# Expert activations of a two-block model: turned on TensorE before the store, or on VectorE after the load

## The reference

```
s1, i1 = top_k(q . sub_keys[0], 16);  s2, i2 = top_k(q . sub_keys[1], 16)
top_s, pos = top_k(s1 + s2, 16);      expert = (i1 * 128 + i2)[pos];  g = softmax(top_s)
u = u_emb[expert];  a = gelu(einsum('thkd,td->thk', u, xb));  coef = g * a
out = einsum('thk,thkd->td', coef, v_emb[expert])
```

## Time and profile before

| | |
|---|---|
| runs | 4169.63, 4172.17, 4174.17 us; median 4172.17 us |
| profiled execution | span 4171.1 us from first to last instruction; its own time lies 1.07 us under the median if measured from the span alone, and no other time of it is given |
| busy share of the span | PE 99%, weight loads 85%, DVE 74%, ACT 55%, POOL 12% |
| chain that ended last | PE 94%, DVE 4%, ACT 1% |
| HBM | 199 GB/s over the span |

### The profile page before, as it was taken

How to read it: one execution, slowest core, us unless ns; L and a number is a source line. 1 busy time by engine, 2 the same in 40 slices (tenths; PEclk the granted TensorE clock), 3 DMA queues, 4 the chain that set the end, 5 groups by cost and what they waited for, 6 DMA issues and landing times.

```text
span 4171.1 us, 72720 instructions
## 1 busy us (share of the span) xinstructions
PE 4116.5 (99%) x21876; PEld 3527.9 (85%) x21876; DVE 3099.3 (74%) x5278; ACT 2278.5 (55%) x4043; POOL 516.1 (12%) x509
## 2 busy tenths in 40 slices
PE   8999999999999999999999999999999999999998
PEld 8978898888888888888889899988888888888887
DVE  6476677885999766777769978688599985566666
ACT  5446544555666655555554465455566665555554
POOL 4100010000222211111100002000022221111110
PEclk9999999999999999999999999999999999999999
DMA  6434656666666666777765545576666666667664
GB/s 223 163 121 150 202 175 194 207 207 197 191 192 191 201 220 219 231 261 246 239 212 178 176 153 184 163 210 206 199 193 190 190 198 221 216 218 238 216 219 161
DMA packets 310247, 831.31 MB, mean 199 GB/s; under 512 B 29040, under 2 KB 129136, under 8 KB 306800
## 3 DMA queue, kind: packets, MB, share of 16 engines
q1 hardware_dynamic: 305184, 812.76, 61.4%
q10 hardware_dynamic: 4944, 17.06, 1.2%
HBM read 779.37 MB, written 50.33 MB: 199 GB/s over the span
## 4 chain that ended last, share of the span: by engine, by line
PE 94%; DVE 4%; ACT 1%; issue 1%; DMA 0%; DVEq 0%; SPq 0%; ACTq 0%
PE psum L419 11%; PE psum L417 11%; PE psum L418 11%; PE psum L485 11%; PE psum L487 11%; PE psum L486 11%; PE psum L1717 5%; PE psum L1719 5%; PE psum L1718 5%; PE psum L1909 2%; PE psum L1911 2%; PE psum L1910 2%; PE psum L408 1%; DVE sb_w_lo L2297 1%; PE psum L426 1%; PE psum L1815 1%
## 5 line engine op out<-in xcount | busy, mean ns | idle before, releaser
L2297 DVE TENSOR_TENSOR sb_w_lo<-sb_raw,sb_w_hi 128x512 fp32r<-128x512 f32 x2736 | 1887.1, 712 | 986.5 <-ACT sb_w_hi L1998 975.5
L1998 ACT CAST sb_w_hi<-sb_raw 128x512 fp32r<-128x512 f32 x2736 | 1696.9, 623 | 1581.2 <-PE psum L487 645.0
L417 PE MATMUL psum<-sb_w_hi,sb_act_hl 128*128 128x512 f32 x2048 | 811.4, 396 | 1.1 <-DVE sb_w_lo L2297 1.1
L419 PE MATMUL psum<-sb_w_lo,sb_act_hl 128*128 128x512 f32 x2048 | 801.5, 391 | 0.0
L418 PE MATMUL psum<-sb_w_hi,sb_act_hl 128*128 128x512 f32 x2048 | 798.9, 390 | 0.0
L485 PE MATMUL psum<-sb_w_hi,sb_act_hl 128*128 128x512 f32 x2048 | 797.0, 389 | 0.8 <-DVE sb_w_lo L2297 0.8
L486 PE MATMUL psum<-sb_w_lo,sb_act_hl 128*128 128x512 f32 x2048 | 796.7, 389 | 0.0
L487 PE MATMUL psum<-sb_w_hi,sb_act_hl 128*128 128x512 f32 x2048 | 796.7, 389 | 0.0
L1717 PE MATMUL psum<-sb_act_hl,sb_w_hi 128*128 128x256 f32 x1488 | 429.8, 289 | 26.9 <-DVE sb_w_lo L2297 13.8
L419 PEld LDWEIGHTS psum<-sb_w_lo,sb_act_hl 128*128 128x128 f32 x2048 | 385.0, 188 | 82.1
L485 PEld LDWEIGHTS psum<-sb_w_hi,sb_act_hl 128*128 128x128 f32 x2048 | 384.4, 188 | 81.0 <-DVE sb_w_lo L2297 1.2
(11 more groups left out here) (377 smaller groups left out, 4240.2 us busy)
## 6 DMA issues: line engine op xcount, KB each, us to landing
sb_raw<-in_u SPq DMA_DIRECT2D x512, 512.0 KB, 4.2
sb_raw<-in_v SPq DMA_DIRECT2D x512, 512.0 KB, 3.5
sb_raw<-in_w_z SPq DMA_DIRECT2D x82, 512.0 KB, 4.3
sb_raw<-in_w_gates SPq DMA_DIRECT2D x64, 512.0 KB, 3.6
sb_acts_in<-acts_mid SPq DMA_DIRECT2D x256, 128.0 KB, 3.3
acts_mid<-sb_acts_out SPq DMA_DIRECT2D x126, 256.0 KB, 5.4
sb_raw<-in_w_proj SPq DMA_DIRECT2D x56, 512.0 KB, 4.2
sb_raw<-in_w_q SPq DMA_DIRECT2D x48, 512.0 KB, 3.8
```

The costliest lines, as they stand in the source:

```text
L417: pe.matmul(ps, h, w_hi[:, c, :], start=k == 0, stop=False)
L419: return pe.matmul(ps, h, w_lo[:, c, :], start=False, stop=k == 15)
L1998: act.copy(w_hi[:, c, :], raw[:, 2 * par + c // 2, (c % 2) * 512:(c % 2) * 512 + 512]).then_inc(hi_ready, 1)
L2297: dve.tensor_tensor(w_lo[:, c, :], raw[:, 2 * par + c // 2, (c % 2) * 512:(c % 2) * 512 + 512], w_hi[:, c, :].bitcast(F32), ALU.subtract). ...
```

## The change

ACT writes the gelu of group g into `up_acts` (both t), SP stores that as it is, in token rows, and no transpose or copy follows in the up-projection. The columns of the up weights are permuted (`expert_rows`, on the host), so that 128 columns hold 4 tiles x 32 experts. In the down-projection one load of 512 KB brings four tiles into one of two slots, so that each of 32x32 blocks only has to be turned inside its 32 partitions; DVE does this for tile i+2 (`turn_tile`) between the low part of tile i and its `w_lo`. The tokens of a tile come out in another order within 128, and `weigh` reads and writes `gate_e` in steps of four elements (16 B). SP's loop over the down-projection is written anew, with one `acts_back` in four tiles.

```diff
-            def turn_acts(g, t, src):
-                pe.wait_ge(tile_out, g * 2 + (e + t + 1))
-                if not isinstance(g, int) or g or blk == 2:
-                    pe.wait_ge(acts_made, g * 2 + (n0 + t - 1))
-                for n in range(4):
-                    mm = pe.transpose(psum[:, 2 + t, n * P:n * P + P], src[:, n * P:n * P + P], ident)
-                mm.then_inc(rows_turned, 1)
-
             def up_tile(g, j):
                 i = g * 4 + j
                 for t in range(QT) if j in (0, 3) else (None,):
                     if j == 0 and not (isinstance(g, int) and g == 0):
-                        turn_acts(g - 1, t, up_acts)
+                        pe.wait_ge(tile_out, g * 2 + (e + t - 1))
...
-            for t in range(QT):
-                turn_acts(31, t, last_acts[:, t, :])
 
             pe.wait_ge(tile_out, evac[f"u{blk}"] + 64)
...
-            def acts_leave(g, t, dst):
-                act.wait_ge(rows_turned, g * 2 + (n0 + t + 9))
...
-                act.copy(dst, psum[:, 2 + t, :]).then_inc(acts_made, 1)
...
+            def turn_tile(i, k):
+
+                slot, n = (k // 4) % 2, k % 4
+                if n == 0:
+                    dve.wait_ge(acts_loaded[slot], (i - k) * 2 + (256 * (blk - 1) + 16))
+                blocks = acts_blocks[slot].rearrange("p (g m) -> p g m", g=8)[:, :, 32 * n:32 * n + 32]
+                dve.transpose(turned_acts[:, k % 2, :].rearrange("p (g x) -> p g x", g=8), blocks).then_inc(acts_turned, 1)
+
+            def lows(i, k, turn=True):
                 dve.wait_ge(c_hi, i + (128 * (blk - 1) + 1))
...
+                if turn:
+                    turn_tile(i + 2, (k + 2) % 8)
+                low(i + b, (b + k) % 2)
+
+            dve.wait_ge(gate_out, GROUPS * blk)
+            turn_tile(0, 0)
+            turn_tile(1, 1)
...
+                sp.wait_ge(tile_out, g * 2 + (evac[f"u{blk}"] + t + 1))
+                to = acts_mid[g, t].rearrange("q p c -> p q c")
+                sp.dma_start(to, src[:, t, :].rearrange("p (q c) -> p q c", q=4)).then_inc(acts_stored[t], 16)
...
+                for t in range(QT):
+                    sp.wait_ge(acts_stored[t], g * 16 + (16 * UP_GROUPS * (blk - 1) + 16))
+                blocks = acts_mid[g].rearrange("t q (x y) c -> (q x) t (y c)", y=4)
+                sp.dma_start(acts_blocks[slot].rearrange("p (t m) -> p t m", t=QT), blocks).then_inc(acts_loaded[slot], 16)
...
                 def weigh(i, slot):
-                    pool.wait_ge(acts_loaded[slot], (i - slot) * 8 + (16 + 1024 * blk))
-                    e = gate_e[:, i, :]
-                    pool.tensor_tensor(e, acts_in[:, slot, :], e, ALU.mult).then_inc(weighed, 1)
+                    pool.wait_ge(acts_turned, i + (128 * blk + 1))
+                    e = gate_e[:, i, :].rearrange("p (t x g) -> p t g x", t=QT, g=4)
+                    turned = turned_acts[:, slot, :].rearrange("p (t g x) -> p t g x", t=QT, g=4)
+                    pool.tensor_tensor(e, turned, e, ALU.mult).then_inc(weighed, 1)
```

More of the change, by code:

```diff
@@ L349, in tiles, with eights @@
                 body(first + 2 * turns, 0)
+        def eights(eng, first, last, body):
+            while first % 8 and first < last:
+                body(first, first % 8)
+                first += 1
+            turns = (last - first) // 8
+            if turns > 0:
+                with eng.Fori(0, turns) as turn:
+                    for k in range(8):
+                        body(turn * 8 + (first + k), k)
+            for i in range(first + 8 * max(turns, 0), last):
+                body(i, i % 8)
         def bank_of(b, first, u):
@@ L478, in out_tile @@
                 for c in range(4):
-                    if first and c == 1:
-                        pe.wait_ge(acts_made, 64 * blk)
                     pe.wait_ge(lo_ready, (i + b) * 4 + c + 1)
@@ L564, in up_tile @@
                     gelu(g - 1, 1, up_acts)
-                    acts_leave(g - 1, 0, acts_out_flat)
-                if j == 1 and not (isinstance(g, int) and g == 0):
-                    acts_leave(g - 1, 1, acts_out_flat)
             def up_hot(g, j):
@@ L1619, in group, with load_down, down_groups, pair @@
                         if j >= 2 and not (isinstance(g, int) and g == 0):
-                            acts_leave(blk, g - 1, j - 2, acts_four)
-                def fetch(i, u, first):
-                    if first == 0:
-                        sp.wait_ge(rows_turned, 2 * UP_GROUPS * blk + 6)
-                        for j in range(2):
-                            acts_back(blk, j, j, blk == 2)
-                    elif first < 127:
-                        acts_back(blk, i + 1, (first + u + 1) % 2, True)
-                    if first == 2:
-                        acts_leave(blk, UP_GROUPS - 1, 0, acts_four)
-                        acts_leave(blk, UP_GROUPS - 1, 1, last_acts[:, 2, :].rearrange("p (n c) -> p n c", n=4))
-                def all_stored():
-                    for t in range(QT):
-                        sp.wait_ge(acts_stored[t], 16 * UP_GROUPS * blk)
+                            acts_leave(blk, g - 1, j - 2, up_acts)
+                down, v = base[f"v{blk}"], a[f"v{blk}"]
+                def load_down(i, k):
+                    for h in range(2):
+                        slot = 2 * ((down + k) % 2) + h
+                        sp.wait_ge(lo_ready, i * 4 + (4 * down + 2 * h - 6))
+                        sp.dma_start(raw[:, slot, :], v[i, h]).then_inc(raw_loaded[slot], 16)
+                def down_groups(first, last):
+                    def pair(g):
+                        for k in range(8):
+                            load_down(g * 4 + k, k)
+                            if k % 4 == 0:
+                                acts_back(blk, g + (k // 4 + 1), 1 - k // 4)
+                    with sp.Fori(0, (last - first) // 2) as turn:
+                        pair(turn * 2 + first)
                 group(0)
@@ L1639, in stream_experts @@
                     group(turn + 1)
+                load_down(0, 0)
                 for t in range(QT):
-                    sp.wait_ge(acts_stored[t], 16 * (UP_GROUPS * blk - UP_GROUPS + 2))
-                stream(f"v{blk}", a[f"v{blk}"], between={64: lambda: residual_back(blk), 110: all_stored, 127: lambda: None}, beside=fetch, apart=3)
+                    sp.wait_ge(acts_stored[t], 16 * (UP_GROUPS * blk - 1))
+                acts_back(blk, 0, 0)
+                load_down(1, 1)
+                sp.wait_ge(hot_ready, GROUPS * blk)
+                sp.wait_ge(gate_out, GROUPS * blk)
+                acts_back(blk, 1, 1)
+                load_down(2, 2)
+                for t in range(QT):
+                    acts_leave(blk, UP_GROUPS - 1, t, last_acts)
+                for i in range(3, 8):
+                    load_down(i, i)
+                    if i == 4:
+                        acts_back(blk, 2, 0)
+                down_groups(2, 16)
+                residual_back(blk)
+                down_groups(16, 30)
+                for i in range(120, 128):
+                    load_down(i, i % 8)
+                    if i == 120:
+                        acts_back(blk, 31, 1)
             def residual_back(blk):
```

66 lines of the change are left out of this document (27 added, 39 removed).

## The result

The changed kernel takes **4117.83 us** (median of 4 runs, 4115.61 to 4118.78) against 4172.9 us for the kernel before, run beside it (median of 4). The ratio is 0.9871, 95% interval 0.9857 to 0.9885: 1.3% faster. The forecast was 4118.6 us. The profiled execution after is the one of 4115.61 us, span 4113.8, so against the span of 4171.1 us it shows 57.3 us less.

The account below looks back on a forecast made before the run. PE, busy 99%, was taken as the bound, so only its queue or waits count. Terms -57.0 - 0.8 + 1.0 + 1.0 + 1.5 + 0.7 = -53.6 us from 4171.1, plus 1.07, gave 4118.6 us; range 4112 to 4130.

Parts of the forecast that it names:

- PE's transposes, -57.0: Both up-projections: 496 transposes leave PE's queue, 62 pairs of groups at 0.92 us each, 57.0 us saved.
- The last pair, -0.8: End of both up-projections: last 16 transposes leave, wait for second gelu stays; 0.4 us saved for each of two, 0.8 us.
- Copies, stores, loads at nothing: ACT loses 128 copies, stores remain 256 KB each, loads of 512 KB land in 3.5 us: no effect on the time.
- Rival B: Entry into each down-projection: late load chain makes PE wait 2 us, lower clock costs 1.5; 7.0 us, 4126; chance 0.12.
- DVE's turn, 0.35 us: Down-projections: 256 added turns of 128x256 take 0.35 us each (0.286 to 0.966), costing nothing in plain tiles.
- POOL's product, 0.74 us: Down-projections: POOL's multiplication follows the turn; if DVE waits, 1.1 of 2.53 us in hand go, nothing lost in plain tiles.
- v1, +1.0: First down-projection: turn and POOL delay tile 43, with 36 and 41 near it; 1.0 us lost (0.3 to 3.3).
- `choose`, +1.0: Up-projection pieces with `choose`: DVE busy 72 of 80 us, some tiles lose cover; 1.0 us lost, both blocks (0 to 4).
- Gate steps, +1.5: Gate steps of the up-projections: DVE comes to 97% of PE's shorter time; 1.5 us lost in both blocks (0 to 16).
- rival A: Gate steps: DVE becomes the bound, meeting POOL's `add_low` in the fourth tile too; 10 to 16 us lost; chance 0.10.
- Tile 56, +0.7: Tile 56 of each up-projection: PE waits for DVE's `w_lo`, so the first group's removal saves nothing; 0.7 us lost.
- Rival C: Down-projections: `weigh` in steps of 16 B holds up DVE's `w_lo`; at 3.0 us, 205 us lost, 4324 us; chance 0.04.

Follow-up runs that it names:

- the repeat: The changed kernel run once more, unaltered, in the same minutes as two further kernels: 4118.03 us, ratio 0.9872 to the kernel before.

## Why the prediction was right, point by point

**PE's transposes, -57.0.** Right. By the gate steps a pair is worth 0.933 us, 62 pairs 57.8; putting the transposes back gave the old pieces of the up-projections to 0.01 us, away from tile 56.

**The last pair, -0.8.** Measured -0.41 and -0.42 in this profile, where PE waits 0.69 us for the second gelu, as the text said; in the repeat nothing is saved (6.73 us, before 6.71). The first profile's fit with 0.4 is in part luck: this entry took 6.29 to 6.73 us in four readings of one kernel.

**Copies, stores, loads at nothing.** Right for the copies and stores, by the same run. The load was mis-sized: 4.99 to 5.87 us at the entries in place of 3.5. Rival B's mechanism came in the repeat, a pause of 1.13 us with the load at its head, and cost 0.4 us a block, not 3.5.

**DVE's turn, 0.35 us.** It takes 0.439 us, nearer to the two-input row of 0.418 than to the cast. The estimate from the Trainium skill, 0.62 us (VectorE: DVE Perf Modes, § The three transpose paths), was further off on the other side. It cost nothing either way, in plain tiles: DVE had 2.53 us in hand and still idles 2.0 us a tile, and the two kernels with more turns put the end of the cover where the rows did.

**POOL's product, 0.74 us.** Wrong size, 1.22 us, with no effect. The step that failed in this term is that I took its time as fixed and asked whether DVE must wait for it: POOL came second and waited for DVE. Of the 0.48 us more, 0.13 us are the steps.

**v1, +1.0.** Measured +1.04 in this profile and +0.36 in the repeat: the step before tile 43 has 6.75 for 6.42 us in both, a turn's 0.33 us, but that before tile 36 has 6.04 us in the one and 5.44 in the other. The part at tile 43 is sure; the rest of this term is within its own scatter, and its near hit is luck.

**`choose`, +1.0.** Too small. 12.5 pairs would be 11.66 us; 10.57 and 10.71 came, so 2.0 us were lost in both blocks together. The place was right (cutting the steps recovers 2.0 us), the count of stalling tiles was a guess.

**Gate steps, +1.5.** Nothing was lost. Here the step that failed is the reading of DVE's busy time. I had 22.9 us a group of DVE's own plus 1.1 more if `add_low` meets DVE in the fourth tile too, 24.0 against PE's 23.7. It does meet it in every tile now, as rival A had it, but the group is then 4 x 5.94 = 23.76 and PE's 23.73, not 24.0 against 23.7. A's mechanism came in full and its price was zero, but only just: with a product of 0.2 us more per tile it was 11 us a block. Where the 0.2 us between 24.0 and 23.76 come from stays open.

**Tile 56, +0.7.** Too small. Over tiles 52 to 60 1.14 us were saved in `u1` and 1.23 in `u2` against the kernel with the transposes back, of 1.87, so 1.4 us lost in both. It was the first group of tile 56 alone that the pause covered, as the text said, but wholly and a little more: the step from tile 55 to 56 is 8.71 and 8.70 us without it and 8.62 and 8.61 with it, while the second group saved 0.46 and 0.52 us. A group is 0.47 us, not 0.35, so this makes 1.1 us of the 1.4. The earlier trace rows show the last part of the pause only; in the kernel before PE had also stood still for 1.13 us ahead of this group of transposes:

```profile
1013.18 0.66 PE L426 MATMUL psum<-sb_consts,sb_acts_in 128*128 128x128 f32 x4 [1.13 <-ACT sb_acts_in L539]
```

**What was not in the sum.** In the profile of before, the low clock followed the pause at tile 56 in both blocks, in that of after in neither, which is 2 x 1.6 = 3.2 us of the 57.3. I had taken the row of that clock for what the pause brings with it; it comes in some executions and not in others. So the spans differ by 3.7 us more than the forecast, and the medians, 4172.17 to 4117.83, by 54.3 us where 53.6 was forecast (55.1 against the 4172.9 us of the same minutes). The closeness owes something to errors that cancel: -0.8 at the pairs, -1.5 at the gate steps, +1.0 at `choose`, +0.7 at tile 56.

**Rival C** was rightly given little: a further 0.8 us of POOL in every tile cost nothing in `v2` and 1.2 us in `v1`. **D** fell with the result.

In short, the step that carried the forecast, PE's queue at 0.92 us a pair, was right and shown by putting the transposes back. The small terms were right in kind and often wrong in size, and their errors cancelled.

## What to carry to other kernels

Where an engine has no idle time, the worth of leaving an instruction out of its queue is the distance between two starts, read from the timeline; here it was forecast to within two per cent (57.0 for 57.8 us). Whether the engine really never waits is read from these distances too, not from its idle time. Before moving work to another engine, price it at its place: what it has in hand per tile there, whether its "busy" contains waiting for another engine, and which instruction it will meet. A stretched instruction (1.51 us on the mean where its kind takes 0.68) is waiting shown as work. A median over a stage's loads says little of the one that opens it (4.9 against 5.87 us). And a pause that the profile shows with a low clock behind it may have none in the next execution, so such a row is a chance and not a term.

## What the runs showed of the hardware that I had not expected

- VectorE at 100% was filled with a reduction of 1.21 us a tile at a cost of 0.01 us a tile, because it took the place of 1.10 us of waiting for POOL; a reduction of 0.67 us cost 0.23 us, and a two-input product of 0.28 us cost 0.18.
- POOL can be kept waiting through several of VectorE's instructions: an addition of 1.34 us took 5.86.
- POOL's product in steps of 16 bytes takes 0.862 us at least, a flat one 0.732.
- The same pause of 2.44 us was followed by 3.41 us at half clock in some executions and not in others, 1.6 us each. Two such places could make 3.2 of the 4.2 us between the changed kernel's runs (4115.61 to 4119.80 us); only two of these runs have a trace, so that is not shown.
- PE's rows can show almost no idle time while it waits: 1.4 us of idle time where 62 tiles took 11.1 us longer, because rows of 0.39 us stand 0.227 us apart.
